# Turning the token rows of the last products on VectorE and by transfers inside SBUF, instead of by TensorE transposes

## What is computed

```
merged = sigmoid(gate_a) * (o_nsa @ w_proj_nsa) + sigmoid(gate_b) * (o_ssm @ w_proj_ssm)
h = h + merged @ w_out
hn = rms_norm(h, norm_mlp_w)
h = h + square(relu(hn @ w_up)) @ w_down        # d_ff = 8192
return rms_norm(h, norm_final_w)
```

## Time and profile before

| | |
|---|---|
| median of 3 runs | 2103.65 us (2103.4 to 2104.85) |
| the profiled execution | 2104.44 us, its span 2102.8 us |
| granted TensorE clock | 0.998 over the span |
| PE busy | 2079.3 us (99%) |
| DVE, ACT, POOL busy | 1310.9 us (62%), 977.7 us (46%), 117.4 us (6%) |
| DMA | 383.59 MB, 182 GB/s on average |

### The profile page before, as it was taken

One profiled execution on the slowest core, in us unless ns is written; L12 is line 12 of the kernel. 1 busy time (PEld: TensorE's weight loads), 2 busy tenths in 40 slices (PEclk: granted clock), 3 DMA queues, 4 the chain that ended last, 5 costly groups with the idle time before them and its releaser, 6 DMA issues.

```text
span 2102.8 us, 28016 instructions
## 1 busy us (share of the span) xinstructions
PE 2079.3 (99%) x9760; PEld 1730.0 (82%) x9760; DVE 1310.9 (62%) x1777; ACT 977.7 (46%) x1319; POOL 117.4 (6%) x165
## 2 busy tenths in 40 slices
PE   8999999999999999999999999999999999999998
PEld 7888888888888888888888878888888888888886
DVE  5565766666655578776678865555545555545554
ACT  5444445454543455554455544544434434433443
POOL 3000000000000011111011100000000000000000
PEclk9999999999999999999999999999999999999999
DMA  8656454545466656666656556566566566656654
GB/s 256 201 161 191 140 173 139 170 142 169 145 205 196 182 173 184 184 183 197 187 168 182 185 202 207 182 181 189 189 194 186 186 194 184 190 192 191 187 191 141
DMA packets 192535, 383.59 MB, mean 182 GB/s; under 512 B 11872, under 2 KB 11968, under 8 KB 191024
## 3 DMA queue, kind: packets, MB, share of 16 engines
q1 hardware_dynamic: 188656, 364.42, 57.0%
q0 software_dynamic: 3600, 17.16, 2.4%
q10 hardware_dynamic: 176, 0.53, 0.1%
HBM read 379.91 MB, written 2.16 MB: 182 GB/s over the span
## 4 chain that ended last, share of the span: by engine, by line
PE 95%; issue 2%; DVE 1%; DMA 0%; ACT 0%; DVEq 0%; POOL 0%; POOLq 0%; SPq 0%; ACTq 0%
PE acc L291 29%; PE acc L293 29%; PE acc L292 29%; PE tr L326 2%; PE x L844 1%; PE x L780 1%; PE x L722 1%; PE tr L802 1%; DVE lo L258 0%; DMA GA<-x 0%; PE x L787 0%; PE tr L804 0%; PE tr L795 0%; PE tr L807 0%; PE x L856 0%
## 5 line engine op out<-in xcount | busy, mean ns | idle before, releaser
L258 DVE TENSOR_TENSOR lo<-raw,hi 128x1024 fp32r<-128x1024 f32 x688 | 844.3, 1235 | 578.2 <-ACT hi L252 566.8
L252 ACT ACTIVATE hi<-raw 128x1024 fp32r<-128x1024 f32 x688 | 721.4, 1059 | 691.5 <-PE acc L293 673.6
L291 PE MATMUL acc<-hi,LAh 128*128 128x512 f32 x1848 | 735.8, 398 | 0.0
L293 PE MATMUL acc<-hi,LAl 128*128 128x512 f32 x1848 | 721.6, 390 | 0.0
L292 PE MATMUL acc<-lo,LAh 128*128 128x512 f32 x1848 | 720.7, 390 | 0.0
L293 PEld LDWEIGHTS acc<-hi,LAl 128*128 128x128 f32 x1848 | 347.3, 188 | 73.5
L291 PEld LDWEIGHTS acc<-hi,LAh 128*128 128x128 f32 x1848 | 347.8, 188 | 72.6 <-issue 1.8
L292 PEld LDWEIGHTS acc<-lo,LAh 128*128 128x128 f32 x1848 | 347.9, 188 | 71.7 <-issue 1.7
L291 PE MATMUL acc<-hi,LBh 128*128 128x512 f32 x896 | 351.8, 393 | 2.7 <-DVE LBl L358 2.7
L292 PE MATMUL acc<-lo,LBh 128*128 128x512 f32 x896 | 349.5, 390 | 0.0
L293 PE MATMUL acc<-hi,LBl 128*128 128x512 f32 x896 | 349.4, 390 | 0.0
(11 more groups left out here) (287 smaller groups left out, 1194.9 us busy)
## 6 DMA issues: line engine op xcount, KB each, us to landing
raw<-w_in SPq DMA_DIRECT2D x304, 512.0 KB, 3.9
raw<-w_up SPq DMA_DIRECT2D x128, 512.0 KB, 3.9
raw<-w_down SPq DMA_DIRECT2D x128, 512.0 KB, 4.5
raw<-w_proj_ssm SPq DMA_DIRECT2D x64, 512.0 KB, 4.4
raw<-w_proj_nsa SPq DMA_DIRECT2D x32, 512.0 KB, 4.7
raw<-w_out SPq DMA_DIRECT2D x32, 512.0 KB, 4.6
W<-acs_rows POOLq DMA_DIRECT2D x8, 1024.0 KB, 5.1
GA<-x SPq DMA_DIRECT2D x4, 512.0 KB, 8.5
```

Source lines behind the costliest of these rows:

```text
L252: act.activation(hi[:, sl, :, :], raw[:, sl, :, :], ACT.Copy).then_inc(s_hi, 1)
L258: dve.tensor_tensor(lo[:, sl, :, :], raw[:, sl, :, :], hi[:, sl, :, :].bitcast(F32), ALU.subtract).then_inc(s_lo, 1)
L291: pe.matmul(o, xh, wh, start=(k == 0), stop=False)
L293: x = pe.matmul(o, xl, wh, start=False, stop=(k == KT - 1))
```

## The change

The 24 turns leave TensorE. In their place, for each:

- DVE turns the rows in blocks of 32x32, two instructions of 128x512 (`turn_blocks`, L365), into one of two buffers: `TB`, new, and half of `W`, a tile of the scan, no longer in use by then. Reading every fourth column makes block rows that fit the next step. This stands right behind the instruction that made the rows.
- GpSimd issues four transfers inside SBUF (`spread_blocks`, L374), each of 32 partitions x 4 KB to 128 partitions x 1 KB, into the other half of `W` (`TS`, a single buffer). It waits for the blocks, and for the event before to have been read (`s_trd`).
- ACT and DVE write high and low parts out of `TS` (`act_split_s`, `dve_split_s`): one instruction each of 128x1024 where there were four of 128x256, except for the residual, which has a weight per feature tile (4 on ACT, 8 of 128x128 on DVE). They do so one hook later than before (3 for 2, 11 for 10), and the last residual turn has moved into the MLP's first chunk, so that the first of the MLP's four iterations is written out of the loop on ACT and DVE.

```diff
+        def turn_blocks(dve, n, src):
+
+            for t in range(2):
+                x = dve.transpose(TBS[n % 2].rearrange("p (b c t j) -> p t c b j", b=4, c=4, t=2)[:, t, :, :, :],
+                                  src[:, t, :].rearrange("p (c i b) -> p c b i", c=4, b=4))
+            x.then_inc(s_tb, 1)
+
+        def spread_blocks(eng, n, read):
+
+            eng.wait_ge(s_tb, n + 1)
+            eng.wait_ge(s_trd, read)
+            for a in range(4):
+                eng.dma_start(TS[:, S * a:S * (a + 1)], TBS[n % 2][32 * a:32 * (a + 1), :].rearrange("i (b n) -> i b n", b=4)).then_inc(s_sp, 16)
+
+        def spread(ct=None):
+
+            v = TS[:, :].rearrange("p (a m j) -> p m a j", a=4, j=32)
+            return v if ct is None else v[:, 2 * ct:2 * ct + 2, :, :]
+
+        def tokens(L, k0, n=4):
+
+            return L[:, k0:k0 + n, :].rearrange("p c (t a j) -> p (c t) a j", t=2, a=4)
+
+        def act_split_s(act, n, Lh, k0, wc=None):
+
+            act.wait_ge(s_sp, 64 * (n + 1))
+            if wc is None:
+                x = act.activation(tokens(Lh, k0), spread(), ACT.Copy)
+            else:
+                for ct in range(4):
+                    x = act.activation(tokens(Lh, k0 + ct, 1), spread(ct), ACT.Copy, scale=wc[:, ct:ct + 1])
+            x.then_inc(s_tra, 2)
+
+        def dve_split_s(dve, e, Lh, Ll, k0, wc=None):
+
+            dve.wait_ge(s_tra, 2 * e + 2)
+            if wc is None:
+                x = dve.tensor_tensor(tokens(Ll, k0), spread(), tokens(Lh, k0).bitcast(F32), ALU.subtract)
+            else:
+                for ct in range(4):
+                    for t in range(2):
+                        x = dve.scalar_tensor_tensor(tokens(Ll, k0 + ct, 1)[:, t, :, :], spread(ct)[:, t, :, :], wc[:, ct:ct + 1],
+                                                     tokens(Lh, k0 + ct, 1)[:, t, :, :].bitcast(F32), ALU.mult, ALU.subtract)
+            x.then_inc(s_trd, 1)
...
+        TB = sb("TB", [P, 2 * NC], c=post)
+        TS = W[:, 0:4, :, :].rearrange("p h c l -> p (h c l)")
+        TBS = (TB[:, :], W[:, 4:8, :, :].rearrange("p h c l -> p (h c l)"))
...
-            pool.wait_ge(s_mg, 4)
+            for n in range(4):
+                spread_blocks(pool, n, E_PB2 + n)
             pool.dma_start(GA[:, 0, :], a["norm_final_w"].partition_broadcast(P)).then_inc(s_wf, 16)
+            for n in range(4):
+                spread_blocks(pool, 4 + n, E_WO + n)
             pool.wait_ge(s_v, 1)
             pool.tensor_tensor(RS[:, 2:4], VV[:, 0:2], mhalf[:, 0:2], ALU.pow).then_inc(s_pow, 1)
+            for n in range(16):
+                spread_blocks(pool, 8 + n, E_MLP + n)
...
-                hooks = {2: [lambda: pe_turn(pe, E_PB2 + n - 1, MG[(n - 1) % 2], [(s_mg, n)])]}
-                mm_chunk(pe, C_PB2 + n, (C_PB2 + n) % 2, LBh, LBl, hooks)
+                mm_chunk(pe, C_PB2 + n, (C_PB2 + n) % 2, LBh, LBl, {})
             for n in range(4):
-                hooks = ({2: [lambda: pe_turn(pe, E_WO + n - 1, H[:, :, NC * (n - 1):NC * n], [(s_acc, C_WO + n)])]} if n
-                         else {2: [lambda: pe_turn(pe, E_PB2 + 3, MG[1], [(s_mg, 4)])]})
-                mm_chunk(pe, C_WO + n, (C_WO + n) % 2, LAh, LAl, hooks, need={6: [(s_trd, E_PB2 + 4)]})
-            pe_turn(pe, E_WO + 3, H[:, :, 3 * NC:4 * NC], [(s_acc, C_WO + 4)])
+                mm_chunk(pe, C_WO + n, (C_WO + n) % 2, LAh, LAl, {}, need={6: [(s_trd, E_PB2 + 4)]})
 
...
-            def mlp(i, last=False):
+            def mlp(i, last=False, first=False):
                 C, e = C_MLP + 8 * i, E_MLP + 4 * i
                 hk = {}
                 for k in range(4):
                     hk[8 * k + 7] = [lambda k=k: take(C + k, (C_MLP + k) % 2, XR[:, 0, :], func=ACT.Relu, scale=RS[:, 2:3])]
-                    hk[8 * k + 10] = [lambda k=k: act_split_t(act, e + k, LAh, 4 * k)]
+                    hk[8 * k + 11] = [lambda k=k: act_split_s(act, 8 + 4 * i + k, LAh, 4 * k)]
...
+                if first:
+                    hk[3] = [lambda: act_split_s(act, 7, LBh, 12, COLS[:, CN2 + 12:CN2 + 16])]
                 slots(act, split_hi, C, 64, hk, last)
 
-            with act.Fori(0, 3) as i:
+            mlp(0, first=True)
+            with act.Fori(1, 3) as i:
...
+            def turn_residual(n):
+                dve.drain()
+                turn_blocks(dve, n, H[:, :, NC * n:NC * (n + 1)])
+
             dve.wait_ge(s_hr, 32)
             for n in range(4):
                 w = COLS[:, CN2 + 4 * n - 4:CN2 + 4 * n]
                 slots(dve, split_lo, C_WO + n, 8,
-                      {2: [lambda: dve_split_t(dve, E_WO + n - 1, LBh, LBl, 4 * n - 4, w) if n else
-                           dve_split_t(dve, E_PB2 + 3, LAh, LAl, 12)],
-                       7: [lambda: add_residual(C_WO + n, (C_WO + n) % 2, n)]})
-            dve_split_t(dve, E_WO + 3, LBh, LBl, 12, COLS[:, CN2 + 12:CN2 + 16])
+                      {3: [lambda: dve_split_s(dve, E_WO + n - 1, LBh, LBl, 4 * n - 4, w) if n else
+                           dve_split_s(dve, E_PB2 + 3, LAh, LAl, 12)],
+                       7: [lambda: add_residual(C_WO + n, (C_WO + n) % 2, n), lambda: turn_residual(n)]})
...
+            def mlp_rows(n, C, par, xa):
 
                 dve.wait_ge(s_xa, xa)
                 dve.tensor_scalar(XR[:, 1, :], acc[par][1][:, :], RS[:, 3:4], 0.0, ALU.mult, ALU.max).then_inc(s_acc, 1)
                 dve.drain()
-                dve.tensor_tensor(Y[:, :, :], XR[:, :, :], XR[:, :, :], ALU.mult).then_inc(s_ff, 1)
+                dve.tensor_tensor(Y[:, :, :], XR[:, :, :], XR[:, :, :], ALU.mult)
+                dve.drain()
+                turn_blocks(dve, n, Y)
```

46 lines of the change are left out of this document (23 added, 23 removed).

## The result

The changed kernel takes **2088.22 us** (median of four runs; three lie between 2087.29 and 2088.95, a fourth took 11963 us and is left out of the ratio), the kernel before 2103.53 us on the same chip (2102.76 to 2104.85). The ratio is 0.9925, 95% interval 0.9908 to 0.9943: 15 us faster. The median of the three others alone is 2087.48 us. The sign was forecast, but the gain is a third smaller than the 22.2 us of the sum, and the time lies 1.2 us above the range of 2080 to 2087 (0.5 us by the three others alone).

A forecast was written before the change was run, and what follows sets the result against it. TensorE was taken as the bound, 95% of the span. 20.5 + 2.5 - 0.8 = 22.2 us off 2104.44 gave 2082.2 profiled, median 2081.5 us; range 2080 to 2087.

The forecast's parts named there:

- Removed: 20.5 + 2.5 us: TensorE from 1240 us: 23 turns at 0.89 us save 20.5; the turn between W_out and MLP saves 2.5.
- E + 9.3: MLP: turned copy lands 9.3 us after chunk end E, at most E + 13.7; no TensorE wait at either bound.
- Block transposes 0.65 us, "the lower bound too": VectorE: each 128x512 f32 block transpose takes 0.65 us, a turn 1.4 with drain; 0.65 also the lower bound.
- Landing 3 us, landed 5.1 us after the turning: Copies inside SBUF: 0.3 wake, 1.8 issuing, 3 landing give 5.1 us after the blocks are turned (4.0 to 9.5).
- The merge's second copy at E + 12.5, nothing lost: Merge's second turn: copy lands 12.5 us after chunk end E, at most E + 14.6; no TensorE loss.
- deadline E + 15.5: Copy may land 15.5 us after chunk end E without delaying TensorE; E + 14.0 in an iteration's last chunk.
- Boundary 0.8 us (0 to 2): Between W_out and MLP: the row factor behind four issues on GpSimd makes TensorE wait 0.8 us, range 0 to 2.
- GpSimd's issues 0.6 us: GpSimd: each transfer issue takes 0.6 us, so the fourth starts 1.8 us after the first.
- rival 1: GpSimd's issues wait for VectorE, 1 us each: sum + 7.5, 2089 us; chance 0.20 with partial losses like it.
- Rival 2: Copies land late, 13 us, 3.8 past the deadline each turn: 70 us lost, 2173 us; 0.08 together with slow block transposes.
- Rivals 3 and 4: 3: slow block transposes, 2131 us at 3 us each, 0.08 with late copies; 4: TensorE no faster, 2103.7 us, 0.02.
- "1.6 around" the span: Whole execution: 1.6 us lie around the profiled span of 2102.8 us in the execution of 2104.44 us.

The follow-up runs named there:

- experiment 4: Changed kernel with block transposes reading their rows in order instead of every fourth element, output not the reference's: 2085.95 us, 0.9921.
- Experiments 8 and 9: Changed kernel with half of the MLP's weights left out (8): 2088.63 us; with one transfer per turn instead of four (9): 2079.92 us; single runs.
- experiment 13: Kernel with two spread buffers and norm factor first, plus a GpSimd filler before the second turn's transfers in each MLP iteration: 2090.25 us, 0.9936.
- Experiment 1: Changed kernel with a second spread buffer, so a turn's transfers wait for the rows two turns back to be read: 2083.73 us, 0.9909.
- Experiment 2: Changed kernel with GpSimd computing the norm's row factor ahead of the last residual turn's transfers: 2087.42 us, 0.9926.
- 15: Kernel with two spread buffers and norm factor first, plus seven drains on idle GpSimd in each MLP iteration: 2080.81 us, 0.9890.

## Why the prediction was right and wrong

- *Removed: 20.5 + 2.5 us.* Right: 0.89 per turn and 21.76 per chunk in the MLP, the W_out chunks too (residual additions 21.76 apart). No turn in the MLP makes TensorE wait: the copies come at E + 12.4 to E + 14.1 over the 16 turns. The sum has them at E + 9.3, with the upper bound at E + 13.7, which two of them pass. The slack swallowed the error there, and not by much: in the iterations' last chunks, where the deadline is E + 14.0, the latest comes at E + 13.6.
- *Block transposes 0.65 us, "the lower bound too".* Wrong by size: 1.04 to 1.13, so that two take 2.1 us, between the 1.3 of the sum and the 2.5 that the prediction also estimated. The strided read was in the diff and had no price. Two of them cost 0.8 us of lateness per turn, and experiment 4 shows their share of the stop at the merge: idle 1.59 instead of 2.67 us.
- *Landing 3 us, landed 5.1 us after the turning.* **This is the step that failed.** The 3 us fit a copy with no weights beside it: each of four in a row lands after 2.5 to 2.8 us at 1380.4, one of 512 KB after 3.1 to 3.5 in the MLP. But there the last of four falls among the weights' transfers: 5.6 in the turn at 1405 us, 6.7 at the merge's second copy, and the copy is there 7.6 us after the turning and not 5.1. The prediction asked whether the copies make the weights late, and not the reverse. Experiments 8 and 9 and the rows at 1380.4 and 1250.7 us show it. The row that could have warned was in the earlier trace rows: four loads issued in a row landed after 5.1 to 13.0 us, and a weight load of 512 KB in the MLP after 3.6 to 6.0. I read the first as a rival of bytes and set it aside for that.
- *The merge's second copy at E + 12.5, nothing lost.* Wrong, E + 18.35. The deadline E + 15.5 was right (2.85 late, 2.82 lost; experiment 13 tries it once more). The late step counts twice here, as with a single buffer the second copy's issue waits for the first copy's landing and reading: reader done at E + 9.4 instead of 7.4, and 8.9 us from there to the copy instead of 5.1. The upper bound of E + 14.6 missed it too: it priced the second landing at 5.1 us instead of 3, but left the reader of the first copy at E + 7.4. Experiment 1 takes out just the second count and gives 4.55 us back.
- *What the sum lacked:* the clock. A stop of 2.67 us cost 2.82 + 1.71. The trace before had this at the scan's end, 2.70 us idle and, four starts later, seven steps of 0.43 us:

```profile
1230.46 0.50 PE L291 MATMUL acc<-hi,LBh 128*128 128x512 f32 x1 [2.70 <-DVE LBl L358]
```

- *Boundary 0.8 us (0 to 2).* 1.3, inside its bounds: the two transposes again (2.1 instead of 1.3) for the most part. Experiment 2 shows the mechanism.
- *GpSimd's issues 0.6 us.* Right, 0.55. None of the 96 takes over 0.59, so rival 1's mechanism (issues that wait for VectorE) is refuted, though it named the merge's second copy as the first to give, and 2089 us; that its number is the nearest is luck. Rival 2 named what happened, copies that land late, but priced it at 13 us; at up to 7.1 only the merge pays. Rivals 3 and 4: no chunk of the MLP pays, and the chunks are 21.76.
- *"1.6 around" the span as a constant, and the same end.* The end's 1.87 us could not be read from any row of before.

The profiled executions: forecast 2082.2, measured 2087.29, 5.1 too low. That is 4.53 at the merge, 0.5 at the boundary and 1.87 at the end, less 1.75 at the start, which is luck. The medians, 2081.5 and 2088.22, lie another 1.6 us apart: the sum put the median 0.8 us below the profiled execution, and it came 0.9 above it. With the merge, the boundary and the end mended (15) the kernel takes 2080.81 us, 22.5 us less than before beside it; the sum without its 0.8 at the boundary was 23.0.
